# Each partition's share of an expert-weight load becomes one run of 16 or 8 KB

## The reference, cut to what matters

```
scores = sigmoid(xt @ w_router); 6 of 64 experts per token, limited to 4 of 8 groups
w      = scores of the chosen / their sum * 2.5
routed[t] = sum over chosen e:  swiglu(xt[t], w_exp_in[e], w_exp_out[e]) * w[t, e]
shared    = swiglu(xt, w_sh_in, w_sh_out)
swiglu(x, w_in, w_out) = (silu(g) * up) @ w_out,  g, up = halves of x @ w_in
```

## Time and profile before

| | |
|---|---|
| median of 3 runs | 2787.89 us (2786.49 to 2792.21) |
| profiled execution: its own time, its span | 2784.83 us, 2783.0 us |
| mean granted TensorE clock | 0.971 of full speed |
| busy: PE, DVE, ACT, POOL | 93%, 55%, 47%, 33% of the span |
| q1 (SP's queue): packets, MB, share of 16 engines' span | 140990, 329.19, 33.8% |
| q0 (POOL's queue): the same | 44832, 132.39, 19.1% |
| HBM read, written | 367.01 MB, 99.22 MB |

### The profile page before, as it was taken

How to read it: one execution, slowest core, us unless ns; L and a number is a source line. 1 busy time by engine, 2 the same in 40 slices (tenths; PEclk the granted TensorE clock), 3 DMA queues, 4 the chain that set the end, 5 groups by cost and what they waited for, 6 DMA issues and landing times.

```text
span 2783.0 us, 38226 instructions
## 1 busy us (share of the span) xinstructions
PE 2581.2 (93%) x12015; PEld 1160.2 (42%) x12016; DVE 1522.5 (55%) x2493; ACT 1316.8 (47%) x1618; POOL 914.5 (33%) x1002
## 2 busy tenths in 40 slices
PE   7999999899999999999889999899999999999980
PEld 2345444555555555545443333233333333333320
DVE  4567455778887668887853333333334333333338
ACT  2354254366665511112115656466565566565645
POOL 3001100100000023333344555455555555554533
PEclk9999999999999999999989999999999999999995
DMA  9530100041101142221148799898797788989848
GB/s 352 193 125 27 46 30 16 11 179 35 35 27 31 35 171 69 76 88 58 46 168 250 215 292 292 241 295 247 219 290 212 220 266 242 287 261 294 256 90 362
DMA packets 185909, 462.69 MB, mean 166 GB/s; under 512 B 21612, under 2 KB 46382, under 8 KB 184142
## 3 DMA queue, kind: packets, MB, share of 16 engines
q1 hardware_dynamic: 140990, 329.19, 33.8%
q0 software_dynamic: 44832, 132.39, 19.1%
HBM read 367.01 MB, written 99.22 MB: 168 GB/s over the span
## 4 chain that ended last, share of the span: by engine, by line
PE 48%; DMA 7%; DVE 5%; issue 3%; SPq 1%; POOL 1%; ACT 0%; DVEq 0%; ACTq 0%; POOLq 0%
PE mx_pH L1316 22%; PE mx_pU L1337 11%; DMA ring<-in_w_exp_in 5%; PE mx_pA L1953 3%; PE mx_pL L1953 3%; PE mx_pH L1978 2%; PE mx_pU L2015 2%; PE mx_pB L1295 1%; PE mx_pB L1986 1%; SPq L1094 1%; DVE ring L1434 1%; DVE ring L1429 1%; DMA qT<-in_w_exp_out 1%; PE mx_pA L1990 0%; PE mx_pU L1963 0%
## 5 line engine op out<-in xcount | busy, mean ns | idle before, releaser
L1316 PE MATMUL mx_pH<-ring,mx_wsi 128*64 x1776 | 809.4, 599 | 36.2 <-DVE mx_h L1229 36.0
L1113 POOL DMA_INDIRECT kT<-s_u,ex_gidx x444 | 444.8, 1002 | 136.9 <-issue 133.6
L1316 PEld LDWEIGHTS mx_pH<-ring,mx_wsi 128*64 128x64 f32 x1776 | 242.0, 139 | 487.4 <-issue 487.4
L1317 PE MATMUL mx_pH<-v,mx_wsi 128*64 128x512 f32 x888 | 410.1, 606 | 0.0
L1337 PE MATMUL mx_pU<-qT,mx_hT 128*64 x896 | 402.9, 592 | 2.3 <-ACT mx_hT L1193 2.3
L1338 PE MATMUL mx_pU<-mx_mrow,mx_hT 128*64 128x512 f32 x896 | 402.8, 592 | 0.0
L1317 PE MATMUL mx_pH<-mx_ln,mx_wsi 128*64 128x512 f32 x888 | 399.2, 592 | 0.0
L1225 DVE STREAM_TRANSPOSE mx_wsi<-kT 128x1024 f32<-128x1024 f32 x112 | 139.2, 1243 | 323.7 <-DMA kT<-s_u,ex_gidx 306.8
L1177 ACT ACTIVATE mx_mrow<-qT 128x2048 f32 x111 | 212.0, 1910 | 153.5 <-PE mx_pU L1338 126.3
L1173 ACT ACTIVATE v<-ring 128x1024 f32 x222 | 222.3, 1048 | 103.3 <-SPq L1079 54.9
L1136 POOL DMA_INDIRECT s_acc<-mx_wso,ex_sidx x112 | 182.9, 1633 | 193.3 <-DVE mx_wso L1252 133.0
(11 more groups left out here) (332 smaller groups left out, 4048.0 us busy)
## 6 DMA issues: line engine op xcount, KB each, us to landing
ring<-in_w_exp_in SPq DMA_DIRECT2D x64, 2048.0 KB
qT<-in_w_exp_out SPq DMA_DIRECT2D x64, 1024.0 KB
fr_wq<-in_w_ada SPq DMA_DIRECT2D x32, 512.0 KB, 5.6
s_acc<-s_acc SPq DMA_DIRECT2D x17, 512.0 KB, 4.1
fr_wf<-in_w_in SPq DMA_DIRECT2D x16, 512.0 KB, 5.8
s_u<-v SPq DMA_DIRECT2D x16, 512.0 KB, 2.6
ring<-s_acc SPq DMA_DIRECT2D x16, 512.0 KB, 14.2
y<-ring SPq DMA_DIRECT2D x16, 512.0 KB, 11.4
```

What stands on the lines that cost most here:

```text
L1113: nc.gpsimd.indirect_dma_start(xg[:, u, g, :], None, u2_q, bass.IndirectOffsetOnAxis(ap=gidx[:, u, g:g + 1].bitcast(U32), axis=0)).then_in ...
L1316: nc.tensor.matmul(pH[low, :], xT[:, u, k, low], wi[:, bass.ds(slot, 1), k, :].rearrange("p a f -> p (a f)"), start=(k == 0), stop=(k == K ...
L1317: m = nc.tensor.matmul(pH[high, :], xT[:, u, k, high], own_in(k, k + 1), start=(k == 0), stop=(k == KD - 1))
```

## The change

Host side, both weight arrays are laid out by partition: w_exp_in[e] as 128 rows of 8 x 512 floats (16 KB), w_exp_out[e] as 128 rows of 2 x 1024 floats (8 KB). Device side, the four places that load them name both sides as two-dimensional, a partition and one contiguous run. The same bytes reach the same places of the tiles. SP issues the same number of DMAs in the same order with the same waits; TensorE, ScalarE, VectorE and GpSimd have no instruction changed.

```diff
         def load_in(r, src):
-            sp.dma_start(wi[:, r, :, :], src).then_inc(w_in[r], 16)
+            sp.dma_start(wi[:, r, :, :].rearrange("p k f -> p (k f)"), src).then_inc(w_in[r], 16)
         def load_out(r, src):
-            sp.dma_start(wo[:, r, :, :], src).then_inc(w_out[r], 16)
+            sp.dma_start(wo[:, r, :, :].rearrange("p c d -> p (c d)"), src).then_inc(w_out[r], 16)
...
-            load_in(r, w_exp_in[r].rearrange("(k p) f -> p k f", p=P))
+            load_in(r, w_exp_in[r])
             out_place(r - 1, 1)
-            load_out(r, w_exp_out[r].rearrange("(c p) d -> p c d", p=P))
+            load_out(r, w_exp_out[r])
...
-                load_in(r, w_exp_in[bass.ds(q * RING + r, 1)].rearrange("a (k p) f -> p (a k) f", p=P))
+                load_in(r, w_exp_in[bass.ds(q * RING + r, 1)].rearrange("a p f -> p (a f)"))
                 out_place((r - 1) % RING, q + 1 if r else q)
-                load_out(r, w_exp_out[bass.ds(q * RING + r, 1)].rearrange("a (c p) d -> p (a c) d", p=P))
+                load_out(r, w_exp_out[bass.ds(q * RING + r, 1)].rearrange("a p f -> p (a f)"))
...
-            sp.dma_start(first_w[:, 0, :, :], exp_weights[0][0].rearrange("(k p) f -> p k f", p=P)).then_inc(w_in_exp[0], 16)
-            sp.dma_start(second_w[:, 0, :, :], exp_weights[1][0].rearrange("(c p) d -> p c d", p=P)).then_inc(w_out_exp[0], 16)
+            sp.dma_start(first_w[:, 0, :, :].rearrange("p k f -> p (k f)"), exp_weights[0][0]).then_inc(w_in_exp[0], 16)
+            sp.dma_start(second_w[:, 0, :, :].rearrange("p c d -> p (c d)"), exp_weights[1][0]).then_inc(w_out_exp[0], 16)
...
-        "w_exp_in": w["w_exp_in"].reshape(N_EXP, 4, KD, 32, 2 * D_E).transpose(0, 2, 1, 3, 4).reshape(N_EXP, D, 2 * D_E), "w_exp_out": w["w_exp_out"], "w_sh_in": w["w_sh_in"], "w_sh_out": w["w_sh_out"],
+        "w_exp_in": w["w_exp_in"].reshape(N_EXP, 4, KD, 32, 2 * D_E).transpose(0, 1, 3, 2, 4).reshape(N_EXP, P, KD * 2 * D_E),
+        "w_exp_out": w["w_exp_out"].reshape(N_EXP, D_E // P, P, D).transpose(0, 2, 1, 3).reshape(N_EXP, P, D_E // P * D), "w_sh_in": w["w_sh_in"], "w_sh_out": w["w_sh_out"],
```

## The result

The changed kernel takes 2811.62 us (median of 4 runs, 2806.03 to 2813.26) against 2787.53 us of the kernel before beside it (4 runs): ratio 1.0080, 95% interval 1.0062 to 1.0098, slower. The forecast was 2777 us and faster; the time is that of the slower rival (2813 us).

A forecast was written before the change was run, and what follows sets the result against it. TensorE was taken as the bound, with about 30 us of holes from weight loads. Shorter holes -15.1, clock -3.4 and slower scatters and gathers +8.0 gave -10.5 us: 2777 us, range 2760 to 2815.

The forecast's parts named there:

- the slower rival: POOL's loop becomes the bound as its rounds beside loads lengthen; 2813 us, from 2790 to 2835; chance 0.36.
- the turns: DMA engines alternate packet by packet between weight queue and GpSimd's queue, whatever the size; a load's row is one packet.
- that rival: Weight loads: 16 KB runs are cut into 4 KB packets, about -8 us, 2780 us; chance 0.04.
- (a): Raw rate of w_exp_in loads: longer runs move faster, 5.4 us before and 4.9 after, 0.5 us a load.
- (b): Turns during w_exp_in loads: fewer packets let fewer GpSimd packets in between; 1.0 us a load, between 0 and 2.6.
- the clock: TensorE after holes: shortened holes give back 1.7 us of slow matmul pairs for two of three, 3.4 us.
- the holes at 2023 and 2176: TensorE idle stretches: the 1.07 us one, made by loads, goes; the 1.43 us one, made by late gathers, stays.
- the 11.44: TensorE's longest idle stretch, in us, behind one late load free of GpSimd's queue; 0.5 us off, staying within 1 us.
- (c): Scatters and gathers wait longer behind larger weight packets, up to 4.2 us per scatter meeting a load; 8 us charged.
- the meeting I expect most often: A scatter meeting the w_exp_out load, its 8 KB packets delaying the scatter by 1.1 us.
- the POOL rival: Other name of the slower rival: POOL's loop decides once a loaded round grows by 1.1 us on average; chance 0.36.
- No change: DMA engines are full and only the order moves: sooner loads push GpSimd's work later; 2786 us, chance 0.15.

The follow-up runs named there:

- in4_out4: Against the kernel before: w_exp_in loaded in 4 KB rows, laid piece after piece by the host, w_exp_out unchanged in 4 KB rows; 2767.67 us, ratio 0.9907.
- the four repeats: Four runs meant to cut the changed kernel's loads into shorter runs, whose packets came out as in the changed kernel; 2806.94 to 2814.99 us.
- in16_out4: Half of the change: w_exp_in in 16 KB runs, w_exp_out as in the kernel before (4 KB rows); 2784.88 us, ratio 0.9979.
- padded: Changed kernel's partition-major layout with 64 floats of padding behind each row, so packets are 2 and 4 KB again; 2783.52 us, ratio 0.9974.

## Why the prediction was wrong

**What bounds the kernel, the turns.** Right. The engines alternate packet by packet, whatever the size: 48 and 52, 80 and 76. The Trainium skill (DMA: Bandwidth & Descriptors, "Queues, rings and completion order") says that a whole packet, typically of 9 to 17 descriptors, goes before the engine changes queue; here a turn was one row of a load against one row of a scatter, as the near-equal counts show. A gather is another matter: its rows are of 1 KB, and GpSimd's data records in the stage are all of 4 KB, 28288 in the kernel before for 111 scatters of 128 and 444 gathers of 32 at the most, so one record holds four gathered rows. Runs of 16 KB were not cut, so that rival falls.

**(a) and (b), the gain of the loads.** Right in direction, and if anything too small. SP's wait fell by 2.8 us a load (10.3 to 7.5) where (a) and (b) gave 1.5. They promised 18.5 us with the clock. What the loads give when POOL is in time is seen best in another kernel: `in4_out4`, in which hardly a scatter is late, gained 22 us between the medians and 26 by the ratio, and in it the holes at 2023 and 2176 are gone and those near 1673, 2417 and 2521 are 1.5, 1.7 and 3.2 us, with the 11.44 at 11.11. How much of this is rate and how much turns was not separated.

**(c), the other side of the turns.** This is the step that failed. It was charged 8 us; to turn a gain of 18.5 to 26 us into a loss of about 22 (0.8% of 2788) it must be 41 to 48 us, an estimate, since its upper end takes the gain from `in4_out4`. The price of one packet was right: 0.64 us for 16 KB and 0.32 for 8 KB were measured, 0.6 and 0.31 assumed. A scatter's eight turns per engine take 8 x 0.97 = 7.8 us beside 16 KB packets instead of 3.4 beside 2 KB, and 5.2 beside 8 KB instead of 4.0 beside 4 KB: 4.3 and 1.2 us more, against the 4.2 and 1.1 of the text. What was wrong was the count. I charged a few new holes, "in each of the four runs of late loads one more", as if each late scatter were an event of its own. But a loaded round of POOL was already over the block (12.07 us against 10.74), so POOL falls behind for as long as loads follow on each other, and what a round gains in length is kept until the stretch ends. Over the block the loaded rounds had 63 us in sum and now have 108. The prediction had both numbers and did not put them together: 1.1 us as the delay at "the meeting I expect most often", and 1.1 us as the growth of a loaded round at which the POOL rival decides. The five rounds above grew by 1.0 us, the loaded rounds of the whole stage by 0.5 on average, and that was enough.

**The clock.** Taken as given back (3.4 us); instead the slow pairs cost 6.8 us more in this execution and 1.9 to 5.4 in the four repeats. A new small hole can bring its own slow pairs (those at 1682.72 and 1709.43 did, those at 1696.12 and 1723.21 did not), so holes that are split up do not give the clock back.

**The slower rival.** Right in mechanism, place and signs: small holes, one a block, transposes that wait for gathers ahead of them, POOL hardly waiting for results in the loaded stretches. That its 2813 us meet the 2811.62 is luck. It took 64 loaded rounds of 12.07 us; with the 48 others that made 1152 us, and with the 133 of waiting for results more than the 1230.5 it had to fit in. Only 47 rounds were loaded. And it had each grow by 1.9 us, where the loaded rounds grew by 0.5 on average. Its condition, a growth of 1.1 us over all loaded rounds, was not met: POOL decides in stretches long before it decides over the stage, where it still waits 91.1 us for results. The argument held against it, that loads which pass sooner meet fewer scatters, hardly shows: POOL waits for a landing 59 times instead of 64, but its loaded rounds are 58 instead of 47.

**No change.** Out for the whole change. For `in16_out4` it describes the time (-0.2%), by another way than the rival's: a gain and a loss that nearly cancel.

## What to carry to other kernels

When two queues share the DMA engines packet by packet, the size of a row is a weight in the sharing: larger rows speed up their own queue and slow the other one. Find what waits for the other queue, compare its round with the block it must keep up with, and if the round is already longer, multiply each packet's delay by all rounds in the stretch. Do this stretch by stretch: an average over the stage hides it. Try the middle size of the row first; here w_exp_in in rows of 4 or 8 KB beat both 2 KB and 16 KB, with w_exp_out left in rows of 4 KB.

## What the runs showed of the hardware

- The size of the packets has an optimum, not a direction: w_exp_in in rows of 2, 4, 8 and 16 KB beside w_exp_out in 4 KB gives ratios of 1, 0.9907, 0.9927 and 0.9979 (the middle two are not told apart).
- A 4 KB packet of the accumulating scatter takes 0.33 us beside each weight row measured (0.327 beside 2 and 4 KB, 0.33 beside 8 and 16 KB), twice the 0.17 us of a 4 KB weight row.
- Dimensions that are contiguous on both sides are joined into one run before a transfer is cut into packets; 64 floats of padding behind each row keep them apart (18 thousand packets against 83 thousand).
- `padded` is 0.26% faster than the kernel before with the same packets. What in the address pattern does this was not tried.
